# Layer one of a two-layer transformer block: two expert pairs share one frame of output rows, and two weight chunks go to homes of their own

## The reference

```python
def hier_moe(h, ...):                     # t: tokens x 1024
    # group: top 1 of 4; expert: top 2 of the 8 in that group; 32 experts in all
    combine = ...                         # tokens x 32, two weights per token, else 0
    a = jnp.einsum('nd,edf->nef', t, w_gate)          # D_FF = 256
    b = jnp.einsum('nd,edf->nef', t, w_up)
    hid = jax.nn.silu(a) * b * combine[:, :, None]
    routed = jnp.einsum('nef,efd->nd', hid, w_down)
    shared = (jax.nn.silu(t @ w_sh_gate) * (t @ w_sh_up)) @ w_sh_down
    return routed + shared
```

## Time and profile before

| | |
|---|---|
| three runs, median (lowest to highest) | 982.12 us (980.53 to 982.19) |
| profiled execution, its own time | 980.76 us |
| its span | 979.0 us |
| PE busy | 921.5 us (94%), 4653 matmuls and transposes |
| DVE busy | 306.7 us (31%) |
| ACT busy | 207.9 us (21%) |
| POOL busy | 23.3 us (2%) |
| read from HBM | 338.07 MB, 346 GB/s over the span |
| granted TensorE clock, mean | 0.991 of 2.4 GHz |

### The profile page before, as it was taken

The page is one execution under the profiler, slowest core; times in us unless marked ns, Lnnn a source line. Parts: engine busy times, 40 slices in busy tenths (PEclk is TensorE's granted clock), DMA queues, the critical chain, the costliest instruction groups (busy, mean ns, idle before and its releaser), DMA issues.

```text
span 979.0 us, 11709 instructions
## 1 busy us (share of the span) xinstructions
PE 921.5 (94%) x4653; PEld 490.1 (50%) x4653; DVE 306.7 (31%) x664; ACT 207.9 (21%) x441; POOL 23.3 (2%) x60
## 2 busy tenths in 40 slices
PE   8999999999999997999999999999998888799986
PEld 5777566556656555866647353333333333333332
DVE  3356367333333334123317132221112122201213
ACT  4233353112112113122423021110011111101112
POOL 4001300000000000000000000000000000000000
PEclk9999999999999998999999999999999999999999
DMA  9950545999999999743377999999999999999995
GB/s 319 391 182 1 196 170 216 421 420 421 419 421 421 420 421 392 286 172 133 101 302 274 409 392 425 426 426 426 428 428 428 428 428 428 428 429 422 421 419 194
DMA packets 55334, 339.86 MB, mean 347 GB/s; under 512 B 9997, under 2 KB 11041, under 8 KB 25970
## 3 DMA queue, kind: packets, MB, share of 16 engines
q1 hardware_dynamic: 49120, 337.07, 84.7%
q10 hardware_dynamic: 5746, 1.91, 0.8%
q0 software_dynamic: 416, 0.16, 0.1%
HBM read 338.07 MB, written 1.05 MB: 346 GB/s over the span
## 4 chain that ended last, share of the span: by engine, by line
PE 77%; DMA 14%; DVE 6%; ACT 2%; issue 1%; SPq 0%; DVEq 0%; ACTq 0%
PE ps L1230 27%; PE ps L1294 13%; PE ps L2395 8%; PE ps L1313 5%; PE ps L2544 5%; DMA ring<-in_expert_w_down_dram 4%; DMA ring<-in_expert_w_gate_dram 4%; PE ps L2611 4%; DMA ring<-in_w_up_dram 2%; DMA ring<-in_expert_w_up_dram 2%; PE ps L2383 1%; PE ps L1136 1%; PE ps L1268 1%; PE ps L1474 1%; PE ps L1694 1%
## 5 line engine op out<-in xcount | busy, mean ns | idle before, releaser
L1230 PE MATMUL ps<-ring,work 128*64 128x256 f32 (+1 forms) x2024 | 337.4, 488 | 11.6 <-DMA ring<-in_expert_w_up_dram 7.1
L1230 PEld LDWEIGHTS ps<-ring,work 128*64 128x64 f32 x2024 | 148.8, 137 | 191.4 <-issue 150.5
L1294 PE MATMUL ps<-ring,work 128*64 128x512 f32 x568 | 131.0, 604 | 6.7 <-DMA ring<-in_expert_w_down_dram 3.8
L970 DVE TENSOR_TENSOR work<-work,ps 128x256 f32<-128x256 f32 (+1 forms) x30 | 16.4, 546 | 264.7 <-PE ps L1230 264.7
L2395 PE MATMUL ps<-xT,ring 128*128 128x256 f32 (+1 forms) x384 | 86.6, 384 | 0.0
L1294 PEld LDWEIGHTS ps<-ring,work 128*64 128x64 f32 x568 | 41.3, 138 | 79.3 <-issue 70.3
L1313 PE MATMUL ps<-parts 128*128 128x512 f32 x248 | 73.5, 420 | 5.6 <-DVE parts L1007 5.6
L2395 PEld LDWEIGHTS ps<-xT,ring 128*128 128x128 f32 x384 | 72.9, 192 | 11.4 <-issue 1.2
L1313 PEld LDWEIGHTS ps<-parts 128*128 128x128 f32 x248 | 42.1, 189 | 40.7 <-issue 17.1
L798 ACT ACTIVATE work<-ps,small 128x512 f32<-128x512 f32 x30 | 20.6, 687 | 195.5 <-PE ps L1294 187.4
L792 ACT ACTIVATE work<-ps 128x256 f32<-128x256 f32 (+1 forms) x31 | 15.1, 487 | 209.7 <-PE ps L1268 209.7
(11 more groups left out here) (391 smaller groups left out, 759.2 us busy)
## 6 DMA issues: line engine op xcount, KB each, us to landing
ring<-in_expert_w_gate_dram SPq DMA_DIRECT2D x20, 2048.0 KB, 17.1
ring<-in_expert_w_up_dram SPq DMA_DIRECT2D x20, 2048.0 KB, 17.3
ring<-in_w_gate_dram SPq DMA_DIRECT2D x32, 1024.0 KB, 17.1
ring<-in_w_up_dram SPq DMA_DIRECT2D x32, 1024.0 KB, 18.6
ring<-in_w_down_dram SPq DMA_DIRECT2D x32, 1024.0 KB, 15.9
ring<-in_expert_w_down_dram SPq DMA_DIRECT2D x16, 2048.0 KB, 18.5
ring<-in_expert_w_gate_dram SPq DMA_DIRECT2D x23, 1024.0 KB, 11.7
ring<-in_expert_w_up_dram SPq DMA_DIRECT2D x22, 1024.0 KB, 11.2
```

Source lines behind the costliest of these rows:

```text
L1230: mm = pe.matmul(ps[CAP * e:CAP * e + CAP, 4 + which, 0:ff], slots, chunks[e][:, k, :], start=(k0 + k == 0), stop=(k0 + k == KC - 1), skip ...
L1294: mm = pe.matmul(ps[CAP * e:CAP * e + CAP, 6 + half, :], hT[:, c0 + k, CAP * e:CAP * e + CAP], columns(chunks[e], k, half), start=(c0 + k ...
```

## The change

It has four parts, all within `m1` but for where the biases are made.

1. **Shared frames.** Pairs 2f and 2f+1 write into the same 64 + 64 rows of banks 6 and 7 (a frame). The windows of the odd pair's experts are moved back by the slot counts of the even pair's (`share_frames`: nine DVE operations on up to 64 columns), so that its tokens lie behind the other's in the frame. `slot_weight` multiplies the hidden rows instead of the outputs, which makes the rows of other experts zero; the weights are thus transposed a pair ahead. The second down adds to the first, and the outputs are taken and scattered once per two pairs: 8 scatters of 8 matmuls instead of 16. ACT writes both high parts straight from PSUM, DVE the low parts. A further pass is now needed when the *sum* of two sharing experts is over 64; MAX_ROUNDS goes from 4 to 5.
2. **Gates ahead.** On PE the gate products of pair n+1 stand between the up products of pair n and the transposes of its hidden rows. The chunk order follows (`FIRST_ORDER`).
3. **Two homes.** The two gate chunks of pair 2 leave the ring for columns of `work` and `last_piece` that are idle until then, by three DMAs which SP issues after `mixed1` (both halves of the mixer's result are in). So 94 chunks go through the ring.
4. **Biases inside the layer.** DVE makes them in pair 4, POOL's iota waits until the homes are used, ACT makes the decays in pair 8. The shared expert's ups and downs go into pairs 8 and 10. The loops over pairs are written out.

The core of the diff (SP, then DVE, ACT and PE):

```diff
+        FIRST_ORDER = [(0, 0), (0, 1)]
+        for p in range(PAIRS):
+            FIRST_ORDER += [(p, 2), (p, 3)] + [(p + 1, j) for j in range(2) if p + 1 < PAIRS] + [(p, 4), (p, 5)]
+            def load_first_homes(cfg):
+                sp.wait_ge(*nth("mixed1", TT))
+                for pair, j in sorted(ASIDE["m1"]):
+                    ...
+                        sp.dma_start(to, src[:, row:row + to.shape[1], :]).then_inc(ev("m1_homes"), 16)
+            def load_first_layer(cfg):
+                for i, (pair, j) in enumerate(FIRST_ORDER):
+                    load_shared(cfg["base"] + i)
+                    if is_aside(cfg, pair, j):
+                        continue
+                    place = place_in_stream(cfg, pair, j)
+                    if place == cfg["base"] + RING:
+                        load_first_homes(cfg)
+                        load_shared_rest()
+                    load(place, pair_chunks(...)[j], 0, 0)
...
+            def weighted_hidden(n, m):
+                dve.wait_ge(ev("sil"), n + 1)
+                dve.wait_ge(*products_done(cfg, m, ups))
+                dve.scalar_tensor_tensor(hs[:, 0:ff], sil[:, 0:ff], slot_weight, ps[:, 5, 0:ff], ALU.mult, ALU.mult)\
+                    .then_inc(ev("h"), 1)
+            def low_parts(n):
+                for half in range(2):
+                    cut = slice(512 * half, 512 * half + 512)
+                    dve.wait_ge(ev("y_parts"), n * 4 + (4 * half - 2))
+                    dve.tensor_tensor(y_low[:, cut].bitcast(F32R), ps[:, 6 + half, :], y_high[:, cut], ALU.subtract)\
+                        .then_inc(ev("y_parts"), 2)
...
+            def take_frame(n, m):                                  # ACT, after odd pairs
+                act.wait_ge(ev("y0p"), n + 1)
+                act.activation(y_high[:, 0:512].bitcast(F32R), ps[:, 6, :], ACT.Copy).then_inc(ev("y_parts"), 2)
+                act.wait_ge(ev("y_parts"), n * 4)
+                act.wait_ge(*products_done(cfg, m, per))
+                act.activation(y_high[:, 512:D].bitcast(F32R), ps[:, 7, :], ACT.Copy).then_inc(ev("y_parts"), 2)
...
+            def first_layer():                                     # PE
+                pe.wait_ge(ev("sh_sil"), TT)
+                products(0, 0)
+                for n in range(PAIRS):
+                    products(1, n)
+                    if n == 0:
+                        turn_weights(0)
+                    if n + 1 < PAIRS:
+                        products(0, n + 1)
+                    scattered = n and n % 2 == 0
+                    if n != SHARED_UP:
+                        turn_hidden(n, bank=4, at=256)
+                    if scattered:
+                        scatter(n - 1, 0, n == 2, False)
+                        scatter(n - 1, 1, n == 2, False)
+                    ...
+                    if n + 1 < PAIRS:
+                        turn_weights(n + 1, bank=5, at=256)
+                    ...
+                    down(getter(n, 0), chunk_used, 4, n, pair=n, part=n % 2)
...
+            chain(dve.tensor_scalar(shared, counts[... even pair ...], float(CAP), None, ALU.min))
+            chain(dve.tensor_tensor(starts, starts, shared, ALU.subtract))
+            dve.tensor_copy(second_pairs(starts_i[:, :]), starts).then_inc(ev("starts_shared"), 1)
```

More of the change, by code:

```diff
@@ L444, in place_in_stream @@
             asides = ASIDE[cfg["tag"]]
+            if cfg["tag"] == "m1":
+                earlier = FIRST_ORDER[:FIRST_ORDER.index((pair, j))]
+                return cfg["base"] + len([c for c in earlier if c not in asides])
             if cfg["tag"] == "m2" and isinstance(pair, int) and pair < 2:
@@ L526, in load_shared_rest @@
                     .then_inc(ev("shared_down_in"), 16)
+            def load_first_layer(cfg):
[7 more added lines that the diff above has]
+                        load_shared_rest()
+                    load(place, pair_chunks(cfg["gate"], cfg["up"], cfg["down"], cfg["ff"], pair)[j], 0, 0)
             def source_of(cfg, name):
@@ new lines, in first_layer @@
+            def first_layer():
+                build_weighted(0, 0)
+                take_weights(0, 0, bank=7, at=0)
+                for n in range(PAIRS):
+                    if n + 1 < PAIRS:
+                        build_weighted(n + 1, n + 1)
+                    if n and n % 2 == 0:
+                        low_parts(n - 1)
+                    weighted_hidden(n, n)
+                    if n == DISTANCES:
+                        distances()
+                    if n == LAGS:
+                        dve.wait_ge(*nth("lag_i_ready", 1))
+                        dve.tensor_copy(dist, dist_i).then_inc(ev("lag_ready"), 1)
+                    if n == SHARED_UP:
+                        take_shared_ups()
+                    if n + 1 < PAIRS:
+                        take_weights(n + 1, (n + 1) % 2)
+                low_parts(PAIRS - 1)
@@ L1029, in moe_vector @@
                         dve.memset(xgP[:, :, SLOTS:SLOTS + CAP], 0.0).then_inc(ev("placed"), 1)
+                share_frames(dve, chain)
             weigh_experts(dve, tag, chain)
@@ L1281, in columns, with down @@
                 return chunk[:, k, 512 * half:512 * half + 512]
-            def down(get, used, j, n, sfx="", pair=None, bank_7=None):
+            def down(get, used, j, n, sfx="", pair=None, bank_7=None, part=None):
                 pe.wait_ge(ev(f"hT{sfx}"), n + 1)
@@ L1329, in get @@
                     for e in range(2):
+                        if tag == "m1" and is_aside(cfg, pair, j + e):
+                            pe.wait_ge(*nth("m1_homes", 48))
+                            views.append(tuple(v.rearrange("p (a b) -> p a b", b=256)
+                                               for v in m1_homes[ASIDE[tag][pair, j + e]]))
+                            continue
                         if is_aside(cfg, pair, j + e):
@@ L1363, in opening, with products @@
                 scatter(n, 1, True, False).then_inc(ev("gathered"), 1)
+            def products(which, n):
+                if which == 0 and n:
+                    pe.wait_ge(ev("xg"), n * 2 + 2)
+                    pe.wait_ge(ev("sil"), n)
+                if which == 1 and n:
+                    pe.wait_ge(ev("scat"), n * 2 + 2)
+                chunks = getter(n, 0)(2 * which, (KC, ff))
+                for k in range(KC):
+                    if which == 0 and n == 0 and k % 4 == 0:
+                        pe.wait_ge(ev("xg"), 1 + k // 4)
+                    for e in range(2):
+                        slots = xgP[:, k, 0:CAP] if n == 0 and e == 0 else xg2[:, n % 2, k, CAP * e:CAP * e + CAP]
+                        mm = pe.matmul(ps[CAP * e:CAP * e + CAP, 4 + which, 0:ff], slots, chunk_row(chunks[e], k),
+                                       start=(k == 0), stop=(k == KC - 1), skip_group_check=True)
+                        if k == KC - 1:
+                            mm.then_inc(ev(HOME_USED[tag]) if is_aside(cfg, n, 2 * which + e) else chunk_used, 1)
@@ L1911, in _ @@
                     .then_inc(ev("attnG_ready"), 1)
-            act.wait_ge(ev("lag_ready"), 1)
-            for hh in range(DH):
-                act.activation(decay[:, hh, :], dist, ACT.Exp, scale=LN_GAMMA[hh]).then_inc(ev("decay_raw"), 1)
             act.wait_ge(ev("lam_a"), 1)
```

234 lines of the change are left out of this document (146 added, 88 removed).

## The result

The changed kernel took 975.34 us as the median of 5 runs (974.32 to 977.34), against 982.12 us before (5 runs, 980.09 to 982.39). The ratio is 0.9938, with a 95% interval of 0.9927 to 0.9948: 0.6% faster. The forecast was 975.3 us.

A forecast was written before the change was run, and what follows sets the result against it. PE and the DMAs were taken as level in m1; 6.6 us off its end makes the span 972.4 and the profiled execution 974.2, and the median's 1.36 more gives 975.5, stated as 975.3, range 971.5 to 980.5.

The forecast's parts named there:

- PE and the DMAs level in m1: In m1, PE eats 6 chunks per 13.0 us, DMAs bring 6 per 15.0; the 12-chunk lead ends with the stage.
- Two homes, 5.0 us: Ring stream of m1: 2 MB moved to idle DMA time at 135.50, so the last chunk lands 5.0 us earlier.
- The early slots: Start of m1's stream: each pair of slots is free 3.5 us or more before it is needed; cost 0.
- share_frames ahead of pair 0: Eleven more DVE operations before pair 0's one-hot, 1.7 to 2.9 us, holding PE up 0 to 0.2; taken as 0.
- Shared frames, 12 us of PE and some 6 us of room: In m1, 8 pairs each 1.5 us shorter on PE, 12.0 in all, showing only as 6 us of room under transfers.
- Tail, 375.7: End of m1: only downs and a scatter follow the last landing at 369.4, ending at 375.7, 6.6 us earlier.
- Biases, 0: Moving distances and decays from the mixer into pairs 4 and 8 gives 0, hidden under PE's products in both places.
- All later marks move along: After m1, layer two's mixer and m2 follow, so every later mark comes 6.6 us earlier.
- The clock: PE in m1 keeps clock 0.96 or more despite short waits; the rival, a fall in the waits, gives 980.4, 4%.
- hand-offs: Rival: PE waits for ACT within each pair of m1; 988.5 at 7%, with half as much 978 to 981 at 7%.
- further pass: Rival: two sharing experts over 64 slots make 96 MB be read again, at least 240 us, giving 1215; 1%.
- the gain isn't there: Rival: homes disturb the gather or m1's stream begins later by their 5 us, giving 980 to 982; 2%.

The follow-up runs named there:

- e3: Kernel before, with the loads of pair 2's two gate chunks cut to 1/32 of their bytes (2 MB less): 981.05 us, ratio 0.9991.
- e1: Changed kernel without the homes, pair 2's two gate chunks back in the ring: 980.32 us, ratio to the kernel before 0.9991.
- e2: Changed kernel with the home loads issued after the first two ring loads of m1: 979.92 us, ratio to the kernel before 0.9988.
- e4: Changed kernel with pair 2's two up chunks cut to 1/32 of their bytes, at the stream's head: 974.55 us, ratio to the kernel before 0.9941.
- e6: Changed kernel with six chunks of pairs 8 and 10 cut to 1/32 (6 MB less): 969.28 us, ratio to the kernel before 0.9872.
- e7: Changed kernel with three useless matmuls on PE in each odd pair of m1: 976.34 us, ratio to the kernel before 0.9955.
- e8: Changed kernel with nine useless matmuls on PE in each odd pair of m1: 986.88 us, ratio to the kernel before 1.0068.
- e10: Changed kernel without homes and with distances, biases and decays made in the mixer as before: 980.29 us, ratio to the kernel before 0.9988.
- e9: Changed kernel without the gates ahead, next pair's gate products behind the downs: 981.25 us, ratio to the kernel before 0.9996.
- e11: Changed kernel with m1's loads from pair 2 on as one 2 MB DMA for two slots: 976.10 us, ratio to the kernel before 0.9939.

## Why the prediction was right, step by step

- *PE and the DMAs level in m1.* Shown: e3 takes bytes and e1 keeps only the saving of PE work, and each alone shortens the stage by 1.0 and 1.2 us.
- *Two homes, 5.0 us.* Shown with its size: e1 gives it back (4.9 of the stage, 5.0 of the median), e2 shows that it is the idle time that pays, the three DMAs went out at 136.06 to 136.91, and the share from 130 to 150 us rose from 0.54 to 0.78.
- *The early slots.* The free slots came at 164.2, 168.1, 172.7 and 176.2 for the 163.6, 167.5, 172 and 175.5 forecast (the whole stage began 0.6 later), and the share is 1.01 from 165 us on. e4 shows how thin this was: with the two loads at the head made light, the DMAs stood still until the next slots at 163.46. The prediction gave it a cost of 0; for a further cut of bytes at that place it would have been the bound.
- *share_frames ahead of pair 0.* Held at 0: the eleven more operations took some 2.1 us of DVE, the one-hot ended at 163.59, and PE's transposes of the weights began at 164.07, with no wait in front.
- *Shared frames, 12 us of PE and some 6 us of room.* 64 instructions went, as counted. PE's downs start 0.98 us after the products in a pair without a scatter (179.52 to 180.50) against 2.50 before: 1.5 per pair, as taken. Over the stage e3 and e6 give 11.0 us. The 6 us of room came out as 5.8 by e6 and 5.9 and 6.0 by e7 and e8.
- *Tail, 375.7.* It ended at 376.73, of which 0.58 is the later start of the stage. The other 0.45 are small shortfalls of the sum. The ups landed when forecast, but the products behind them took 3.70 us where 3.5 stood in the sum (the earlier trace rows has 3.67), the hidden rows' way 1.63 (368.64 to 370.27) for 1.5, and the steps behind the downs some 0.1 more than reckoned. The last downs landed at 369.9, as forecast on the later start, and ACT's copy ended at 370.22, so they waited for the copy and not for the ring, as "just in time" had put it. The stage is 6.2 us shorter instead of 6.6.
- *Biases, 0.* Shown by e10.
- *All later marks move along.* Only roughly. In the two profiles the end of `m1` is 5.6 us earlier, the router's products ahead of `m2` 6.5, the first products of `m2` 4.8, the end of the span 4.4. The first two differ by the clock: PE's first block of products in layer two's mixer took 14.95 us before and 14.05 after, and before, the granted clock was 0.52 from 388 to 392 us, where that block begins, and 1.00 from 392. The later loss is told in the last section.
- *The number.* That 975.34 lies within 0.1 us of 975.3 is luck. The stage gave 6.2 us and not 6.6, the medians differ by 6.8, with 5.1 to 7.2 as the interval, and the five runs of the changed kernel spread over 3 us.
- *The clock.* It stayed at 1.00 in every stretch of `m1` read above, with PE waits of up to 1.32 us, at the closest one every 5 us, and PE busier than forecast: 8.7 to 9.2 of 10 us, for 12.2 of 15. The Trainium skill (TensorE: Matmul & The Clock Gate, "HAM oscillation") describes a PE that falls to half rate in each wait for transfers, where the work between two waits is shorter than the wait. Here the work was the longer of the two, and the fall did not come. The rivals *hand-offs*, *further pass* and *the gain isn't there* did not happen either; *faster transfers* neither: 419 to 423 GB/s.

## What to carry to other kernels

Where an engine and the DMAs are level, cutting either alone gives little; find out by how much each would lead without the other, and cut both by that much. Move bytes to times when the DMAs are idle, not merely to another buffer, and look at both ends of the stream: at its head free slots bind, at its tail the work that needs the last chunk. An edit that saves an engine 11 us and shows 1 us has still made room, and a filling of useless work measures how much.

## What the runs showed of the hardware

The spread of the changed kernel's five runs goes with the granted clock: they had spans of 972.6 us at a mean clock of 0.993, 973.6 and 973.5 at 0.989, 974.6 and 975.5 at 0.986. The clock is not the whole of it: of the runs of the kernel before in the set of e9 to e11, one had a span of 978.2 us and one of 982.3, both at 0.993. In the profiled execution after, a loss is seen ahead of `m2`, where twelve matmuls of no use (24 in the trace) stand between the router's products and the slot counts. First the kernel after, timeline of PE:

```profile
514.82 5.47 PE L1965 MATMUL ps<-ones,ident 128*128 128x128 f32 x24
519.94 0.37 PE L1904 MATMUL ps<-routed_r,counters 128*128 128x32 f32 x1
```

The same place in the kernel before:

```profile
520.72 2.92 PE L1766 MATMUL ps<-ones,ident 128*128 128x128 f32 x24
524.93 0.26 PE L1705 MATMUL ps<-routed_r,counters 128*128 128x32 f32 x1 [1.29 <-DVE routed_r L1612]
```

At full clock they take 2.92 us and PE then waits 1.29 us for DVE; in the later profile they took 5.47 us, near twice as much, and the next matmul came without a wait. The stretch around it tells the same, clock 0.83 for PE busy 19.86 of 20 us:

```profile
505.00:525.00 20.00, 19.86 (x124) 17.78 (x123) 10.05 (x34) 6.32 (x11) 0.00 (x0) 0.83 0.86 335
```

From 514 to 520 us the clock was 0.50, its lower level, although PE had hardly stood still: from 505 to 510 us it was busy for 5.00 of 5 us at clock 1.00, from 510 to 512 for 1.86 of 2. What it did just before the fall was transposes and the router's products of 36 columns. From the start of these products to the first products of `m2` it took 15.5 us (510.66 to 526.15), before 13.8 (517.15 to 530.92): 1.7 us of the 2.4 by which this profile's gain falls short of the medians'.

The other traces say that this is not one execution's chance alone. The same 24 records took 2.92 us in both traces of the old order (before, e3), and 4.37 to 5.47 in all eleven of the changed kernel and its variants, among them the one without homes and with the biases in the mixer (e10) and the one without the gates ahead (e9). From the start of the router's products to the first slot count it took 7.78 us in the two, 7.87 to 7.99 in five of the eleven (e4, e6, e7, e9, e11), and 9.13 to 9.50 in six. So the fall goes with what all eleven share, the frames among it, and costs 0.1 to 1.7 us of the change's gain where it comes; two traces of the old order are few, and what brings it about was not shown.
